# Twelve modulation blocks of the last mixer layer made in the even layer's attention instead of the recurrent layer

## The chip, the cores and the metric

The kernel runs on one core of one Trainium2 chip. The core has five engines that run side by side and wait for each other through semaphores: TensorE (PE, matmuls into the eight PSUM banks), VectorE (DVE), ScalarE (ACT), GpSimd (POOL) and SyncE (SP), which here issues the weight loads. The metric is the device time of one execution in microseconds, as the median of several.

## The reference

Everything is float32. A token stream x of 256 x 1024 goes through two blocks one after the other. The first has a recurrent mixer layer (a WKV-7 group of 8 heads of 64, and a gated delta rule group of 4 heads of 128, in chunks of 64 tokens), an MLP, a banded attention and a second MLP. The second block has an even mixer layer (neighbourhood attention on 8 heads and differential attention on 4 pairs of heads), a convolutional FFN, an odd mixer layer (grouped-query attention and a long convolution) and a last FFN; it also carries 256 context tokens. What matters here is how the second block is modulated:

```python
for layer in range(DEPTH):
    mod_l = (jax.nn.silu(c) @ w_ada[layer] + b_ada[layer])[:, None, :]
    mod_c = jax.nn.silu(c_ctx) @ w_ada[layer] + b_ada[layer]
    sh1_l, sc1_l, g1_l, sh2_l, sc2_l, g2_l = jnp.split(mod_l, 6, axis=-1)
```

`c` and `c_ctx` are inputs. So both layers' modulation vectors (6 x 1024 numbers for x and for the context) depend on nothing that the network computes and may be made at any time before their use. Layer 0's are first used when the second block starts, layer 1's only at the end of the FFN of layer 0, ahead of the odd mixer.

## The kernel before

**Weights.** All weights come from memory in blocks of up to 128 x 4096 numbers (2 MB) through a ring of three slots (`RING = 3`). `weight_plan` (L127) lists their order; SP issues them in that order, each as soon as PE has let go of the block three places earlier (L3292), and `weight` (L316) checks that PE takes them in that same order. An order changed in one place must be changed in the other.

**Modulation.** Each layer's `w_ada` is 12 blocks, `ada0` to `ada11` for layer 0 and `ada12` to `ada23` for layer 1. `pe_ada(j)` (L1021) multiplies one block by silu(c) and silu(c_ctx) with eight matmuls that use 32 columns of the array each, in four row strips; `dve_ada(j)` (L1032) adds the bank to the tile ADR. After twelve of them `pe_mod` (L1043) sums and turns ADR with four small matmuls, and `dve_mod` (L1051) adds the bias and writes the tile MODF. Their matmuls depend on nothing but the ring, and all 24 are written by hand between steps of the recurrent layer (`pe_mix`, `dve_mix`).

**The recurrent layer's end.** A triangular inverse is made in five steps k = 1 to 5 (L1353) for two groups g: matmuls "LX" (copied out by ACT), then "XLX" and "XLXt" (added by DVE, which then makes the masked operand of the next LX). Behind it come "ub" and "wb", and then four chunks c (L1378), each with `pe_bchunk_in` (state times queries) and `pe_bchunk_out` (state update and output), with DVE between the two. Blocks 11 to 16 stand in and behind the inverse, 17 to 23 in the chunks. Then `pe_eout` (L1996) turns the result y and multiplies it by the output projection, `pe_mod(1)` between the two.

**The even layer's attention.** `pe_pairs` (L753) runs 24 steps, twelve of neighbourhood attention (two with an added table and one without in each group of three, and an output product of 16 matmul records after each group) and twelve of differential attention. Step i issues the scores of step i, then what `between[i]` holds, then the transposes of step i-2 and the output product of step i-3. DVE (`dve_pairs`, L830) takes maxima, normalizes, copies half of the transposes; ACT takes exponentials and copies the other half.

**PSUM banks.** `open_bank` (L300) gives a result its bank. Without a number it takes the next in rotation, and in each case PE waits until the bank's last content has been read:

```python
            if b is None:
                b = state["bank"] % 8
                state["bank"] += 1
            if state["last"][b]:
                reader, n = marks.get("read " + state["last"][b], (scalar_done, 0))
                pe.wait_ge(reader, n)
```

In `pe_pairs` the scores have fixed banks 0 to 3, the transposes 4 to 6 and the outputs 7 (6 and 7 in the differential half), whatever the rotation stands at. Two scores are opened together before either is computed.

Of the kernel before, what the change touches and what calls it, by code (L numbers as in the profile page):

```python
# [126 lines left out]
def weight_plan():  # L127

    plan = []
    plan += [("lora_in", 8 * 256), ("rkv1", 4096), ("rkv0", 4096), ("lora_out", 3 * 512), ("rkv2", 4096)]  # L130
    ada = [(f"ada{j // 12}.{j % 12}", 4096) for j in range(24)]
    plan += [("bqkv0", 4096)] + ada[0:2] + [("bqkv1", 4096), ("bqkv2", 4096), ("bgate", 4096), ("bab", 64)] + ada[2:]
    plan += [(f"eout{i}", 4096) for i in range(2)]

    def mlp(i):
        return ([(f"up{i}.{n}", 4096) for n in range(8)] + [(f"down{i}.{h}.{n}", 4096) for n in range(4) for h in range(2)]
                + [(f"pproj{i}", 2048)] + [(f"pgate{i}.{h}", 4096) for h in range(2)])

    def ffn(i):
        return ([(f"cup{i}.{n}", 4096) for n in range(11)]  # L140
                + [(f"cdown{i}.{s}.{h}.{n}", 4096 if n < 2 else 3072) for s in range(2 - i) for n in range(3) for h in range(2)])

    plan += mlp(0) + [(f"qkv{i}", 4096) for i in range(6)] + [(f"aout{i}", 4096) for i in range(2)] + mlp(1)
    plan += [(f"win{i}", 4096) for i in (3, 4, 0, 1, 2, 5)] + [(f"wout{i}", 4096) for i in range(2)] + ffn(0)
    plan += [("hin1", 4096), ("hfilter", 3 * 64 + 1024), ("hin2", 4096), ("gq", 4096), ("gkv", 8 * 256), ("hin0", 4096)]
    plan += [(f"oout{i}", 4096) for i in range(2)] + ffn(1)
    return plan
# [65 lines left out]
def build(nc, T, out, counts):  # L213

    with ExitStack() as ctx:
# [64 lines left out]
        SM = small  # L280
# [966 lines left out]
        def pe_mix():  # L1247
# [105 lines left out]
            for k in range(1, 6):  # L1353
# [4 lines left out]
                if k < 3:  # L1358
                    pe_chunk_out(k + 1)
                pe_ada(10 + k)  # L1360
                for g in range(2):
                    pe_xlx("gdn", k, g, LX2, XT2)
                if k == 1:
                    pe_mod(0)
            pe_ada(16)
            pe.wait_ge(vector_done, at("gdn ready"))
# [11 lines left out]
            for c in range(4):  # L1378
                if c > 0:
                    pe_ada(16 + 2 * c)  # L1380
                    pe_bchunk_in(c)
                pe_ada(17 + 2 * c)
                pe_bchunk_out(c)
# [250 lines left out]
        def dve_mix():  # L1634
# [167 lines left out]
            for k in range(1, 6):  # L1802
                if k < 3:
                    dve.wait_ge(vector_done, dve.n)
                    dve_chunk_in(k + 1)
                    dve_chunk_out(k + 1)
                dve_ada(10 + k)
                for g in range(2):
# [23 lines left out]
            for c in range(4):  # L1832
                if c > 0:
                    dve_ada(16 + 2 * c)
                dve_bchunk_in(c)
                if c == 0:
                    dve_ada(16)
                if c == 1:
                    dve_y_affine()
                if c == 2:  # L1840
                    dve_y_out()
                dve_ada(17 + 2 * c)
                dve_bchunk_out(c)
                if c == 0:
                    dve_y_scale()
                dve.wait_ge(vector_done, dve.n)
# [13 lines left out]
            dve.mark("yb src")  # L1860
            dve_mod(1)

# [133 lines left out]
        def pe_eout():  # L1996
            ws, pss = [], {}
            for h, (Y, src) in enumerate(((YA, "ya src"), (YB, "yb src"))):
                pe.wait_ge(vector_done, at(src))
                for t in range(2):  # L2000
                    pe_turn(f"ymix turned {t}.{h}", [Y[:, t, i * P:(i + 1) * P] for i in range(4)])
                if h == 0:
                    pe_mod(1)
                for t in range(2):
# [306 lines left out]
        junk512 = ar.take(512)  # L2311
# [387 lines left out]
        def pe_even():  # L2699
# [61 lines left out]
            pe.wait_ge(loaded["bias"], at("bm loaded"))  # L2761
            pe_pairs("even", even_steps, PB5)

# [103 lines left out]
        def dve_even():  # L2867
# [66 lines left out]
            dve.wait_ge(vector_done, dve.n)  # L2934
            dve_pairs("even", even_steps, PB5, LAMR[:, 4:5], SM[:, 152:168], junk512)
            dve.mark("subln sums")
# [579 lines left out]
```

## Time and profile before

| | us |
|---|---|
| median of 3 runs | 2123.4 (2119.75 to 2123.53) |
| the profiled execution | 2126.54 |
| its span on the core | 2124.7 |
| mean granted clock, as a share of the full clock | 0.991 |

The profile is of one execution. Its span is the time between its first and last instruction, 1.8 us under that execution's time. Engine times are busy times inside the span: PE is the matmul side of TensorE, PEld its weight loads. A "releaser" is the event that ended an engine's wait. Matmuls are pipelined, a matmul appears as two records here, and their ends are modelled, so the starts carry more than the durations.

### The profile page before, as it was taken

The page shows a single profiled execution, that of the slowest core. Times are in us where ns is not written, and L with a number is a line of the kernel's source. Part 1 is how long each engine was busy: PE and PEld are TensorE (multiplying, and loading weights), DVE is VectorE, ACT ScalarE, POOL GpSimd, SP SyncE. Part 2 cuts the span into 40 slices and gives each one's busy share as a digit, 9 for nine tenths or more (in the row PEclk, how much of TensorE's full clock was granted, in tenths as well). Part 3 has the DMA queues.
Part 4 walks back from the last instruction along what each step waited for, and adds up shares of the span by engine and source line. Part 5 has one row for each costly group of instructions (what it writes and reads, how often), then busy time and mean ns, then how long its engine had stood idle before and what let it go on. Part 6 is the DMA issues. An engine that isn't in the chain of part 4 may idle for free.

```text
span 2124.7 us, 25115 instructions
## 1 busy us (share of the span) xinstructions
PE 2068.8 (97%) x10948; PEld 1468.0 (69%) x10948; DVE 1152.4 (54%) x1642; ACT 389.4 (18%) x787; POOL 10.8 (1%) x22
## 2 busy tenths in 40 slices
PE   8999999999999999999999999999999999999998
PEld 7887674895467589545864556988874466559963
DVE  2643765664521466643444764555555765646765
ACT  2313110100031410004112642111110012321110
POOL 0000000000000000000000000000000000000000
PEclk9999999999999999999999999999999999999999
DMA  5323777445343244534231102122223353124441
GB/s 199 120 120 131 296 268 328 178 178 214 138 177 140 80 174 159 188 148 163 80 119 40 40 1 80 45 110 84 108 91 138 148 212 139 40 80 159 159 163 75
DMA packets 22749, 292.69 MB, mean 138 GB/s; under 512 B 2752, under 2 KB 3008, under 8 KB 4848
## 3 DMA queue, kind: packets, MB, share of 16 engines
q1 hardware_dynamic: 20864, 280.67, 34.8%
q0 software_dynamic: 1776, 10.43, 1.3%
q8 instruction: 86, 1.41, 0.3%
q14 instruction: 23, 0.19, 0.0%
HBM read 290.03 MB, written 1.05 MB: 137 GB/s over the span
## 4 chain that ended last, share of the span: by engine, by line
PE 88%; DVE 8%; DMA 2%; ACT 1%; issue 1%; SPq 0%; DVEq 0%; ACTq 0%
PE bank L324 86%; DMA ring<-in_W 2%; PE bank L685 1%; DVE small L848 1%; DVE arena L869 1%; DVE arena L639 1%; DVE arena L862 0%; DVE arena L1016 0%; PE bank L778 0%; DMA X<-in_x 0%; DVE arena L2560 0%; DVE arena L696 0%; DVE arena L843 0%; DVE HT L2436 0%; DVE arena L488 0%
## 5 line engine op out<-in xcount | busy, mean ns | idle before, releaser
L324 PE MATMUL bank<-arena 128*128 128x128 f32 (+9 forms) x3856 | 679.5, 350 | 7.3 <-DVE arena L1008 2.5
L324 PEld LDWEIGHTS bank<-arena 128*128 128x128 f32 (+3 forms) x3856 | 474.3, 183 | 197.8 <-issue 159.0
L324 PE MATMUL bank<-HT,ring 128*128 128x128 f32 (+1 forms) x2672 | 453.7, 328 | 3.5 <-DMA ring<-in_W 1.8
L324 PEld LDWEIGHTS bank<-HT,ring 128*128 128x128 f32 x2672 | 403.6, 191 | 48.1 <-issue 9.5
L324 PE MATMUL bank<-ring,arena 128*128 128x512 f32 x690 | 307.4, 600 | 7.6 <-DVE arena L470 7.0
L324 PEld LDWEIGHTS bank<-ring,arena 128*128 128x128 f32 x690 | 131.4, 192 | 170.1 <-issue 169.8
L324 PE MATMUL bank<-ring,HT 128*128 128x512 f32 (+2 forms) x512 | 192.6, 533 | 2.4 <-DMA ring<-in_W 1.4
L324 PE MATMUL bank<-arena,ring 128*128 128x128 f32 (+2 forms) x1046 | 172.4, 322 | 0.8 <-issue 0.8
L694 ACT ACTIVATE arena<-bank 128x512 f32<-128x512 f32 (+2 forms) x127 | 69.7, 571 | 532.2 <-PE bank L324 502.0
L324 PEld LDWEIGHTS bank<-arena,ring 128*128 128x128 f32 (+1 forms) x1046 | 152.9, 191 | 13.9 <-issue 2.2
L324 PEld LDWEIGHTS bank<-ring,HT 128*128 128x128 f32 x512 | 89.3, 190 | 101.2 <-issue 95.9
L324 PE MATMUL bank<-HT,arena 128*128 128x128 f32 (+3 forms) x704 | 111.9, 323 | 0.0
L324 PEld LDWEIGHTS bank<-HT,arena 128*128 128x128 f32 (+1 forms) x704 | 98.3, 189 | 9.5 <-issue 2.6
L483 DVE TENSOR_TENSOR arena<-ring 128x2048 f32<-128x2048 f32 (+1 forms) x17 | 37.3, 2192 | 61.7 <-PE bank L324 61.7
L595 DVE TENSOR_TENSOR arena<-ring 128x2048 f32<-128x2048 f32 (+1 forms) x35 | 64.6, 1860 | 4.3 <-DMA ring<-in_W 4.0
L627 DVE TENSOR_TENSOR ADR<-ADR,bank 128x512 f32<-128x512 f32 x17 | 11.7, 688 | 89.9 <-PE bank L324 89.9
L2560 DVE SCALAR_TENSOR_TENSOR arena<-arena,CP 128x512 f32<-128x512 f32 (+1 forms) x88 | 54.4, 618 | 3.1
L632 DVE TENSOR_TENSOR arena<-ADR,bank 128x512 f32<-128x512 f32 x34 | 23.4, 687 | 58.4 <-PE bank L324 58.4
L324 PE MATMUL bank<-ring,SCW 128*32 128x512 f32 x384 | 50.7, 652 | 4.1 <-DMA ring<-in_W 3.4
L812 ACT ACTIVATE arena<-bank,small 128x512 f32<-128x512 f32 (+1 forms) x80 | 47.3, 599 | 35.4 <-DVE small L848 27.8
L616 ACT ACTIVATE arena<-bank 128x512 f32<-128x512 f32 x37 | 22.0, 595 | 159.1 <-PE bank L324 110.5
L778 PE MATMUL bank<-KC,arena 128*128 128x128 f32 x256 | 39.0, 282 | 10.7 <-DVE arena L862 5.2
(299 smaller groups left out, 1540.0 us busy)
## 6 DMA issues: line engine op xcount, KB each, us to landing
ring<-in_W SPq DMA_DIRECT2D x125, 2048.0 KB, 7.7
ring<-in_W SPq DMA_DIRECT2D x6, 1536.0 KB, 8.7
ring<-in_W SPq DMA_DIRECT2D x4, 1024.0 KB, 9.0
arena<-in_rel POOLq DMA_DIRECT2D x1, 2048.0 KB, 11.0
arena<-in_rpb POOLq DMA_DIRECT2D x1, 2048.0 KB, 9.2
arena<-in_dft POOLq DMA_DIRECT2D x2, 640.0 KB, 7.0
X<-in_x SPq DMA_DIRECT2D x2, 512.0 KB, 5.6
X<-in_ctx POOLq DMA_DIRECT2D x1, 1024.0 KB, 5.7
```

The costliest lines, as they stand in the source:

```text
L324: return nc.tensor.matmul(out_, lhsT, rhs, start=start, stop=stop, skip_group_check=True)
L483: tt(T1, B12, B11, ALU.subtract).then_inc(vector_done, dve.one())
L595: tt(d, a, b, op).then_inc(vector_done, dve.one())
L616: activation(dst, PS[banks.get(f"{label} {'x' if j == 1 else 'z'}{q}", 0)][:, :], ACT.Copy).then_inc(scalar_done, act.one())
L632: tt(dst, view(U), view(full(dve, f"{label} {c}{q}")[:, :]), ALU.add).then_inc(vector_done, dve.one())
L639: tt(dst, a, b, o).then_inc(vector_done, dve.one())
L685: last = nc.tensor.transpose(ps[:, i * P:(i + 1) * P], s, K("ident"))
L694: nc.scalar.activation(dst, s, ACT.Copy).then_inc(e.done, e.one())
L778: last = nc.tensor.transpose(ps[:, c * P:(c + 1) * P], PB[:, j % 3, s, a:a + P], K("ident"))
L812: activation(PB[:, i % 3, s, a:b], src, ACT.Exp, bias=st[:, c:c + 1], scale=sign, accum_out=st[:, 4 + c:5 + c]).then_inc(scalar_done, act. ...
L848: nc.vector.tensor_reduce(st[:, s * np_:(s + 1) * np_], ps[:, 0:w].rearrange("p (a c) -> p a c", a=np_), AX.X, ALU.max, negate=True).then_ ...
L2560: stt(c, raw[:, :, x:x + SEQ], C(f"fconv_w{i}", 22 * x + m), c, ALU.mult, ALU.add).then_inc(vector_done, dve.one())
```

## The change

The twelve blocks of layer 1 (`ada12` to `ada23`) leave the recurrent layer. `weight_plan` puts them between the last input weight of the even layer and the first output weight `wout0`. In `pe_pairs` and `dve_pairs` of the even attention they are handed in as `between`: blocks 12 and 13 in step 0, then one block each in steps 1, 2, 3, 4, 6, 7, 9, 10, 12 and 13. They take fixed banks, 7, and 6 for block 13. `pe_mod(1)` follows the attention on PE, `dve_mod(1)` on DVE. In the recurrent layer only `ada11` stays in the inverse, in step 1. The number of matmuls, of DVE instructions and of bytes loaded is the same as before.

```diff
@@ -129,7 +129,7 @@
     plan = []
     plan += [("lora_in", 8 * 256), ("rkv1", 4096), ("rkv0", 4096), ("lora_out", 3 * 512), ("rkv2", 4096)]
     ada = [(f"ada{j // 12}.{j % 12}", 4096) for j in range(24)]
-    plan += [("bqkv0", 4096)] + ada[0:2] + [("bqkv1", 4096), ("bqkv2", 4096), ("bgate", 4096), ("bab", 64)] + ada[2:]
+    plan += [("bqkv0", 4096)] + ada[0:2] + [("bqkv1", 4096), ("bqkv2", 4096), ("bgate", 4096), ("bab", 64)] + ada[2:12]
     plan += [(f"eout{i}", 4096) for i in range(2)]
 
     def mlp(i):
@@ -141,7 +141,7 @@
                 + [(f"cdown{i}.{s}.{h}.{n}", 4096 if n < 2 else 3072) for s in range(2 - i) for n in range(3) for h in range(2)])
 
     plan += mlp(0) + [(f"qkv{i}", 4096) for i in range(6)] + [(f"aout{i}", 4096) for i in range(2)] + mlp(1)
-    plan += [(f"win{i}", 4096) for i in (3, 4, 0, 1, 2, 5)] + [(f"wout{i}", 4096) for i in range(2)] + ffn(0)
+    plan += [(f"win{i}", 4096) for i in (3, 4, 0, 1, 2, 5)] + ada[12:] + [(f"wout{i}", 4096) for i in range(2)] + ffn(0)
     plan += [("hin1", 4096), ("hfilter", 3 * 64 + 1024), ("hin2", 4096), ("gq", 4096), ("gkv", 8 * 256), ("hin0", 4096)]
     plan += [(f"oout{i}", 4096) for i in range(2)] + ffn(1)
     return plan
@@ -1357,12 +1357,12 @@
                     pe_lx("gdn", k, g, MASKED2, XI2)
                 if k < 3:
                     pe_chunk_out(k + 1)
-                pe_ada(10 + k)
+                if k == 1:
+                    pe_ada(11)
                 for g in range(2):
                     pe_xlx("gdn", k, g, LX2, XT2)
                 if k == 1:
                     pe_mod(0)
-            pe_ada(16)
             pe.wait_ge(vector_done, at("gdn ready"))
             for t in range(2):
                 ps = open_bank(f"ub{t}")
@@ -1377,9 +1377,7 @@
                 pe.mark(f"wb{t}")
             for c in range(4):
                 if c > 0:
-                    pe_ada(16 + 2 * c)
                     pe_bchunk_in(c)
-                pe_ada(17 + 2 * c)
                 pe_bchunk_out(c)
 
         def act_keep(n, i, dst, h):
@@ -1804,7 +1802,8 @@
                     dve.wait_ge(vector_done, dve.n)
                     dve_chunk_in(k + 1)
                     dve_chunk_out(k + 1)
-                dve_ada(10 + k)
+                if k == 1:
+                    dve_ada(11)
                 for g in range(2):
                     dve_grow("gdn", k, g, XI2, XT2)
                     if k < 5:
@@ -1830,16 +1829,11 @@
                 copy_out(dve, f"wb{t}", WT[:, 4 * t:4 * t + 4, :], lambda ps: k4(ps[:, :]))
             dve.wait_ge(vector_done, dve.n)
             for c in range(4):
-                if c > 0:
-                    dve_ada(16 + 2 * c)
                 dve_bchunk_in(c)
-                if c == 0:
-                    dve_ada(16)
                 if c == 1:
                     dve_y_affine()
                 if c == 2:
                     dve_y_out()
-                dve_ada(17 + 2 * c)
                 dve_bchunk_out(c)
                 if c == 0:
                     dve_y_scale()
@@ -1858,7 +1852,6 @@
             dve.wait_ge(vector_done, dve.n)
             tt(YB, YB, GB, ALU.mult).then_inc(vector_done, dve.one())
             dve.mark("yb src")
-            dve_mod(1)
 
 
         def pe_norm_sum(label, tiles):
@@ -1999,8 +1992,6 @@
                 pe.wait_ge(vector_done, at(src))
                 for t in range(2):
                     pe_turn(f"ymix turned {t}.{h}", [Y[:, t, i * P:(i + 1) * P] for i in range(4)])
-                if h == 0:
-                    pe_mod(1)
                 for t in range(2):
                     pe.wait_ge(scalar_done, at(f"read ymix turned {t}.{h}"))
                 for t in range(2):
@@ -2759,7 +2750,15 @@
                     spread("kn")
             pe.wait_ge(vector_done, at("even heads"))
             pe.wait_ge(loaded["bias"], at("bm loaded"))
-            pe_pairs("even", even_steps, PB5)
+            blocks = {i: [12 + n] for n, i in enumerate((0, 1, 2, 3, 4, 6, 7, 9, 10, 12, 13), 1)}
+            blocks[0].insert(0, 12)
+
+            def modulation(i):
+                for n, j in enumerate(blocks[i]):
+                    pe_ada(j, 7 - n)
+
+            pe_pairs("even", even_steps, PB5, {i: lambda i=i: modulation(i) for i in blocks})
+            pe_mod(1)
 
             w = weight("wout0").rearrange("p (k c) -> p k c", k=KT)
             pss = [open_bank(f"wout0.{t}") for t in range(4)]
@@ -2932,7 +2931,15 @@
             dve.wait_ge(vector_done, dve.n)
             ts(LAMR[:, 4:5], LAMR[:, 4:5], -(0.8 - 0.6), None, ALU.add).then_inc(vector_done, dve.one())
             dve.wait_ge(vector_done, dve.n)
-            dve_pairs("even", even_steps, PB5, LAMR[:, 4:5], SM[:, 152:168], junk512)
+            rows_of = {i: 12 + n for n, i in enumerate((0, 1, 2, 3, 4, 6, 7, 9, 10, 12, 13), 1)}
+
+            def modulation(i):
+                if i == 0:
+                    dve_ada(12)
+                dve_ada(rows_of[i])
+
+            dve_pairs("even", even_steps, PB5, LAMR[:, 4:5], SM[:, 152:168], junk512, {i: lambda i=i: modulation(i) for i in rows_of})
+            dve_mod(1)
             dve.mark("subln sums")
             dve.wait_ge(scalar_done, at("subln root"))
             nc.vector.reciprocal(SM[:, 152:168], SM[:, 152:168]).then_inc(vector_done, dve.one())
```

## Rows read from the trace of the kernel before

**Rows 1.** Part 1 of the page: busy us (share of the span) x instructions.

```profile
PE 2068.8 (97%) x10948; PEld 1468.0 (69%) x10948; DVE 1152.4 (54%) x1642; ACT 389.4 (18%) x787; POOL 10.8 (1%) x22
```

**Rows 2.** Windows of four stages: length, busy by engine, PEclk, DMA share, GB/s.

```profile
284.00:309.00 25.00, 22.50 (x184) 17.54 (x176) 19.12 (x29) 2.99 (x5) 0.00 (x0) 1.00 0.68 252
319.00:348.00 29.00, 27.73 (x217) 14.52 (x216) 20.92 (x32) 0.00 (x0) 0.00 (x0) 0.94 1.00 422
1169.00:1216.00 47.00, 45.67 (x258) 25.79 (x256) 37.33 (x88) 29.78 (x87) 0.00 (x0) 1.00 0.13 46
1216.00:1253.00 37.00, 31.81 (x209) 21.77 (x210) 32.76 (x101) 24.89 (x73) 0.00 (x0) 1.00 0.01 1
```

**Rows 3.** Tile SCW, whole run: durations min/median/max in ns, starts, forms.

```profile
L324 PE MATMUL bank<-ring,SCW x384: 592/592/1063, 94.1 to 346.5; 128*32 128x512 f32 x192
```

**Rows 4.** PE's timeline around inverse steps: start, us, instructions, [idle before].

```profile
300.39 1.92 PE L324 MATMUL bank<-ring,SCW 128*32 128x512 f32 x16
302.25 3.84 PE L324 MATMUL bank<-arena 128*128 128x128 f32 x32
306.28 1.16 PE L324 MATMUL bank<-arena 128*128 128x128 f32 x8 [0.19 <-DVE arena L1008]
...
315.23 1.16 PE L324 MATMUL bank<-X,arena 128*128 128x128 f32 x8 [0.31 <-DVE arena L1016]
```

**Rows 5.** Chain that ended last, 260 to 370: start, us, what.

```profile
308.06 1.23 DVE small L1573
...
313.29 0.69 DVE ADR L1040
...
328.68 11.04 DMA ring<-in_W
...
343.40 11.57 DMA ring<-in_W
...
355.01 10.57 PE bank L324 x24
```

**Rows 6.** DVE's lines of code in 319 to 348: count, busy us, mean ns.

```profile
L1040 DVE TENSOR_TENSOR ADR<-ADR,bank 128x512 f32<-128x512 f32 x8 | 5.5, 687 | 6.3 <-PE bank L324 5.9
```

**Rows 7.** PE's timeline, the end of the recurrent layer.

```profile
339.77 3.56 PE L324 MATMUL bank<-ring,SCW 128*32 128x512 f32 x16 [0.87 <-DMA ring<-in_W]
...
348.02 1.09 PE L685 MATMUL bank<-KC,arena 128*128 128x128 f32 x8
```

**Rows 8.** PE's timeline in the even attention.

```profile
1169.56 1.13 PE L324 MATMUL bank<-arena 64*128 64x512 f32 x4
...
1175.41 1.09 PE L778 MATMUL bank<-KC,arena 128*128 128x128 f32 x8 [0.45 <-DVE arena L869]
...
1183.62 1.39 PE L778 MATMUL bank<-KC,arena 128*128 128x128 f32 x8
...
1216.40 0.66 PE L778 MATMUL bank<-KC,arena 128*128 128x128 f32 x4 [0.95 <-DVE arena L862]
```

**Rows 9.** DVE's timeline in the even attention.

```profile
1220.98 1.29 DVE L848 TENSOR_REDUCE small<-bank 128x1 f32<-128x512 f32 x2 [1.73 <-PE bank L324]
```

**Rows 10.** DMA issues in 1165 to 1185: KB each, us to landing.

```profile
ring<-in_W SPq DMA_DIRECT2D x1, 2048.0 KB, 7.6
```

**Rows 11.** Timelines around the band attention: PE twice, then ACT.

```profile
700.30 1.58 PE L324 MATMUL bank<-arena 64*128 64x256 f32 x16
...
731.41 19.12 PE L324 MATMUL bank<-ring,arena 128*128 128x512 f32 x44 [0.57 <-ACT arena L694]
...
700.40 0.60 ACT L694 ACTIVATE arena<-bank 128x512 f32<-128x512 f32 x1 [7.54 <-PE bank L324]
```

**Rows 12.** Timelines ahead of the GQA attention: PE, then DVE.

```profile
1837.07 13.24 PE L324 MATMUL bank<-arena 64*128 64x512 f32 x52
...
1838.24 0.87 DVE L3194 SCALAR_TENSOR_TENSOR arena<-bank,CP,arena 128x255 f32<-128x255 f32 x2 [2.29 <-PE bank L324]
1839.14 0.87 DVE L3198 SCALAR_TENSOR_TENSOR arena<-bank,CP,arena 128x255 f32<-128x255 f32 x2
```

## Prediction

> **What bounds the kernel now.** I read the totals first: TensorE is called busy for 2068.8 of 2124.7 us, VectorE for 1152.4 [rows 1]. A share that high says only that a stage must be read from inside, so next come the windows of the two places that the change touches [rows 2]. In the inverse's steps (284 to 309) PE is busy 22.5 of 25.0 us and DVE 19.12. In the four chunk steps (319 to 348) PE is busy 27.73 of 29 us, DVE 20.92, and the DMA share is 1.00 at 422 GB/s: the stream of weight blocks is full there. In the first half of the even attention (1169 to 1216) PE is busy 45.67 of 47 us and DVE 37.33; in the second half PE has 31.81 and DVE 32.76 of 37, and the DMA engines are almost still (46 and 1 GB/s). So the blocks leave a place where the DMA engines are full and go to one where they are empty. The question is whether PE has room there. The timelines and the chain of waits answer that, and after them the waits for PSUM banks.
>
> **What one block costs.** Each of the 24 blocks is 8 matmuls (16 records) of 592 ns, overlapping each other [rows 3]. Start to start a block takes PE 302.25 - 300.39 = 1.86 us [rows 4]. On DVE it is one add of 687 ns [rows 6].
>
> **Removed from the inverse.** In steps 2, 3 and 4 a block stands between the LX and the XLX matmuls. PE's waits lie elsewhere, before the next LX, 0.19 us on DVE [rows 4], so nothing late is uncovered: the copies of LX on ACT take about 0.6 us, and LX of group 1 and XLX of group 0 cover them. DVE's products come 1.86 us earlier with PE's. Each block is worth 1.86: 5.6 us. After step 4 DVE does the mean and variance of y from 308.06 until the add of block 15 at 313.29, an add of 0.69 [rows 5]. That work does not shrink, so blocks 15 and 16 give only about 0.7 us. The matmuls of "ub0", at 315.23 before [rows 4], start about 6.3 us earlier, at 308.9.
>
> **Removed from the chunk steps.** Blocks 17 to 23 go. Of DVE's 20.92 us [rows 2], 5.5 are eight adds [rows 6]; 15.4 remain. DVE waits for PE's products four times (two state products and two "vn" or "ob", about 1.15 us each, estimated as half of a PE piece of the 27.73 us: 4.6 in all); two copies of 0.7 lie beside PE; the handovers make some 1.0. That is 15.4 + 4.6 - 1.4 + 1.0 = 19.6 us where there were 29.0. The stage turns from bound by blocks to bound by DVE; gain 9.4 more, 15.7 in all. Behind it, the transposes of y (348.02 before [rows 7]) start at about 332.3. Then the waits for DMA go: the chain of waits runs through the ring for 11.04 us before 339.7 and for 11.57 before 355 [rows 5], and the output projection starts its second weight only at 355.01. With eout0, eout1 and up0.0 fetched early, the projection's first half ends about 17.4 us earlier than before. This holds another 1.7 us for two short waits and the `pe_mod` of four small matmuls. DVE's norm of YB then ends at about 340, the half projection at 348, so it stays covered. Bounds: 12 us (only the 6.3, and the chunk steps kept at DVE's pace of 20.92 plus 4.6) and 19 us. **Recurrent layer: -17.4.**
>
> **Added to the attention.** Twelve blocks. Are they in gaps? In the first twelve steps PE's pieces follow each other without idle but for 0.45 us at 1175.41 [rows 8]; transposes that stretch to 1.39 us instead of 1.09 [rows 8] hide about 0.3 more, in each of three groups. So a block is paid nearly in full. Ten blocks stand in steps 0 to 10: 10 x 1.86 = 18.6, less 0.45 and 3 x 0.3: 17.25. Blocks 22 and 23 stand in steps 12 and 13, where PE waited 0.95 us for DVE before the transposes at 1216.40 [rows 8]; they fill that, and DVE, which had 1.73 us of idle before 1220.98 [rows 9], takes its two adds without loss: 3.7 - 0.95 - 0.55 (stretched transposes, PE and DVE drawn side by side) = 2.2, plus 0.3 because block 23 wants bank 7 before DVE has read block 22: 2.5. No block beside attention steps is in this trace, so the bounds are wide: DVE's 0.69 each (8.3 us) if PE had room, 1.92 each plus waits (23 us) if not. I take the upper end, as the PE rows show no room.
>
> **The ring in the attention.** It has three slots. Blocks 12 and 13 are there at step 0, which starts at 1169.56 [rows 8]. Block 14 takes the slot of win5, free at that moment, and one load alone takes 7.6 us from issue to landing [rows 10]: 1177.2. Scores with a table take two pieces like the 1.13 us of 1169.56 (1.06 start to start), those without one, so step 1 ends its scores at 1169.56 + 2.1 + 3.7 + 2.1 = 1177.4, just after. Block 15 is issued when block 12 is done (1173.5), and the DMA engines need about 5.0 us a block when full (2.1 MB at 422 GB/s [rows 2]). It lands near 1182.2 but is wanted at 1177.4 + 1.86 + 1.06 = 1180.3: 1.9 us, with 0.1 for block 16. Later ones are in time, since a step and its block take at least 5.0 us. **+2.0** (0 to 4). `pe_mod(1)` then stands alone on PE before wout0: **+0.9**. DVE's add of the bias runs beside wout0. Sum for the attention: 17.25 + 2.5 + 2.0 + 0.9 = **+22.6**.
>
> **What is moved without being named: PSUM banks.** `open_bank` hands out banks in rotation and waits for the last reader. Thirteen rotating opens go before the even attention (blocks 12 to 23 and mod1), and one comes back after it. So every rotating bank is 3 further on between eout and wout0, and 4 further on after. Among themselves that changes nothing; it matters where a fixed bank follows, in `pe_pairs`. Counted through the program, three places change. (a) Band attention: the second score bank (1) is now that of "v1.0", copied by ACT from 700.40 for 0.60 us, while the scores started at 700.30 [rows 11]: +0.75. The first output bank is no longer that of the last head, for which PE waited 0.57 us at 731.41 [rows 11]: -0.6. (b) Even attention: wout0 opens banks 4 to 7, 7 being the last output that DVE reads; `pe_mod` covers it: 0. (c) GQA attention: bank 1 is now that of "hu.1", which DVE reads in the convolution until 1839.14 + 0.87 = 1840.0, while PE's scores started at 1837.07, the head of 13.24 us without a gap [rows 12]: **+2.9** (between 0, if PE catches up in its later waits, and 3.0). I take the top, since DVE's next waits are for PE. Together **+3.1**.
>
> **Sum.** -17.4 + 22.6 + 3.1 = **+8.3 us**. The profiled run took 2126.5 us (span 2124.7), 3.1 over the median of 2123.4; the difference is applied to the median: **2131.7 us**, 0.39% slower.
>
> **Rivals.**
> A. *The blocks are hidden in the attention* (the other side). DVE is nearly as full as PE there (37.33 of 47 us), and if PE's busy time is stretched by the way its ends are modelled, a block costs DVE's 0.69: 8.3 + 0.9 = 9.2 instead of 22.6, so -5.1: 2118.3. It decides when a block costs under about 0.8 us. For it: LDWEIGHTS are far from full, 25.79 of 47 us [rows 2]. Against: PE's pieces start one behind the other with no idle but what is named above [rows 8]. The Trainium skill bears on this: its page Perfetto Trace Analysis (section Identifying the Most-Contended Engine) holds that matmul busy time is a poor measure and that LDWEIGHTS' share shows the headroom. By that rule the attention has 45% free, and this rival would be right. Chance 0.07.
> B. *The bank and ring waits come to nothing*: PE's later gaps in GQA take up the wait, and block 15 lands in time. 8.3 - 3.1 - 2.0 = +3.2: 2126.6. For it: one load's 7.6 us is a single sample. Chance 0.17.
> C. *PE's clock falls where the fillers go.* The granted clock stood at half level (1.2 of 2.4 GHz) when block 22 ran, 3.56 us for 1.92, after a short wait for DMA [rows 7]; that 1.6 us is in my gain. In the chunk steps PE would be busy some 70% with gaps of up to 2 us. If it falls there, PE's 4.6 us on the path double and the projection's start loses 1.6: +6.2 on top of 8.3: 2137.9. Against: in the second half of the even attention, with PE at 31.81 of 37 us, the granted clock is 1.00 [rows 2]. The Trainium skill, page TensorE: Matmul & The Clock Gate (section HAM oscillation), warns that gaps between groups of matmuls let the clock fall, so that fillers are worth more than their time. [...] Chance 0.18.
> Forecast: 0.58. That the change does not do what it says is excluded by the code: all twelve blocks leave.
>
> **Numbers.** Within 0.2% is 4.2 us, about what a measurement of this kernel can tell from no change: 2119.2 to 2127.6. The forecast and C are slower (0.76), B is the same (0.17), A faster (0.07). The range leaves out A and covers B, C and the bounds of the ring and of the chunk steps: 2124.5 to 2139.
>
> **What would show it.** In the profile after: "ub0" about 6 us earlier; the chunk steps at 20 us; no DMA wait from 280 to 350; then the start of the even attention 17 us earlier (less 0.15), its length 84 to 105 us; a wait of 2 us on the ring at step 2; and a wait of PE on DVE's convolution of 2.9 us ahead of the GQA scores. What would make it wrong: a block in the attention that costs much less than 1.86, a longer wait on the ring, or a half clock in either place.

## The result and the profile after

The changed kernel takes 2144.35 us (median of four executions, 2140.44 to 2144.99) against 2123.47 us for the kernel before beside it (2119.75 to 2124.13): ratio 1.0098, interval 1.0081 to 1.0116, or +20.9 us. Forecast were +8.3 us and a range that ended at 2139. The direction was right, the size was not. The profiled execution took 2140.44 us (span 2138.6), 13.9 us over that of before.

The totals say little, as [rows 1] did: the same work in a longer span.

```profile
PE 2070.5 (97%) x10948; PEld 1473.0 (69%) x10948; DVE 1154.7 (54%) x1642; ACT 390.1 (18%) x787; POOL 10.7 (1%) x22
```

The windows of the four stages (columns as in [rows 2]): inverse steps, chunk steps, first and second half of the even attention.

```profile
284.00:304.00 20.00, 17.20 (x140) 15.87 (x138) 18.39 (x27) 4.87 (x7) 0.00 (x0) 1.00 0.01 1
312.73:333.46 20.73, 16.10 (x104) 13.88 (x105) 15.51 (x24) 0.00 (x0) 0.00 (x0) 0.84 0.00 1
1153.60:1207.00 53.40, 50.58 (x329) 23.06 (x328) 34.21 (x73) 22.27 (x63) 0.00 (x0) 1.00 0.90 364
1207.00:1261.50 54.50, 49.28 (x337) 30.10 (x336) 46.17 (x131) 33.39 (x95) 0.00 (x0) 1.00 0.38 146
```

The DMA stream has moved: from 1.00 in the chunk steps to 0.00, and from 0.13 in the attention to 0.90. The chunk steps last 20.7 us where they lasted 29 [rows 2, 7], and DVE is busy 15.5 us of them, as worked out (15.4). But their mean granted clock is 0.84 where it was 0.94, as a share of 2.4 GHz; half clock is the lower of its two levels, 1.2 GHz. PE's timeline of the recurrent layer's end (start, us, instructions, [idle before <- releaser]) shows where:

```profile
276.36 8.90 PE L324 MATMUL bank<-arena 64*64 64x64 f32 x112
...
300.70 3.00 PE L324 MATMUL bank<-arena 128*128 128x128 f32 x24 [0.64 <-DVE arena L1008]
307.26 1.90 PE L324 MATMUL bank<-X,arena 128*128 128x128 f32 x8 [3.55 <-DVE arena L1016]
308.96 1.91 PE L324 MATMUL bank<-arena 128*128 128x128 f32 x8
310.66 1.17 PE L324 MATMUL bank<-X,arena 128*128 128x128 f32 x8
...
313.96 4.06 PE L324 MATMUL bank<-arena 64*128 64x128 f32 x32 [1.24 <-DVE arena L1610]
320.19 3.13 PE L324 MATMUL bank<-arena 64*128 64x128 f32 x16 [2.17 <-DVE arena L1613]
323.95 5.96 PE L324 MATMUL bank<-arena 128*64 128x128 f32 x32 [0.63 <-DVE arena L1627]
330.51 3.02 PE L324 MATMUL bank<-arena 128*64 128x128 f32 x24 [0.60 <-DVE arena L1627]
333.46 1.09 PE L685 MATMUL bank<-KC,arena 128*128 128x128 f32 x8
...
349.21 1.04 PE L685 MATMUL bank<-KC,arena 128*128 128x128 f32 x8
```

"ub0", the piece at 307.26, takes 1.90 us where it took 1.16 [rows 4]: behind a wait of 3.55 us PE works at half clock, and again behind one of 2.17 us. No wait in these rows is for DMA any more. I measure this **recurrent stage** from the first piece behind mod0 to the transposes of YB: 349.21 - 276.36 = 72.85 us. Before, in the rows below, it was 365.42 - 277.78 = 87.64. So it gave 14.8 us.

```profile
277.78 5.13 PE L324 MATMUL bank<-arena 64*64 64x64 f32 x80
...
365.42 1.04 PE L685 MATMUL bank<-KC,arena 128*128 128x128 f32 x8
```

PE's timeline of the even attention, after:

```profile
1153.61 1.13 PE L324 MATMUL bank<-arena 64*128 64x512 f32 x4
1154.67 1.13 PE L324 MATMUL bank<-arena,KC 128*128 128x256 f32 x4
1155.73 3.64 PE L324 MATMUL bank<-ring,SCW 128*32 128x512 f32 x32
...
1161.66 1.92 PE L324 MATMUL bank<-ring,SCW 128*32 128x512 f32 x16 [0.17 <-DMA ring<-in_W]
1163.51 1.14 PE L324 MATMUL bank<-arena 64*128 64x256 f32 x8
1166.54 1.93 PE L324 MATMUL bank<-ring,SCW 128*32 128x512 f32 x16 [1.89 <-DMA ring<-in_W]
...
1177.44 1.92 PE L324 MATMUL bank<-ring,SCW 128*32 128x512 f32 x16 [0.68 <-DMA ring<-in_W]
...
1220.29 1.93 PE L324 MATMUL bank<-ring,SCW 128*32 128x512 f32 x16 [0.45 <-DVE ADR L1040]
...
1260.59 0.98 PE L324 MATMUL bank<-KC,ADR 128*128 128x32 f32 x8
1261.55 0.67 PE L324 MATMUL bank<-ring,arena 128*128 128x512 f32 x1
```

From its first scores to wout0 it lasts 1261.55 - 1153.61 = 107.94 us. Before, it lasted 1252.81 - 1169.56 [rows 8] = 83.25 us, so +24.7. Of the rows below, the second is the start of wout0 before; the first is the longest wait of its second half.

```profile
1248.09 0.66 PE L778 MATMUL bank<-KC,arena 128*128 128x128 f32 x4 [1.36 <-DVE arena L862]
...
1252.81 3.60 PE L324 MATMUL bank<-ring,arena 128*128 128x512 f32 x8
```

The ring wait of 1.89 us at step 2 is where it was expected. Those of 0.17 at step 1 and 0.68 at step 4 were not expected; with 0.15 ahead of block 16 they make 2.9 us. The last place is the GQA attention, PE and then DVE:

```profile
1849.14 14.88 PE L324 MATMUL bank<-arena 64*128 64x512 f32 x52 [3.02 <-DVE arena L3205]
```

```profile
1848.12 0.87 DVE L3205 SCALAR_TENSOR_TENSOR arena<-bank,CP,arena 128x255 f32<-128x255 f32 x2
```

The wait for the bank is 3.02 us (forecast 2.9), but the piece behind it takes 14.88 us where it took 13.24 [rows 12]: half clock again, 1.64 us more. In the band attention a wait of 0.78 us came and 0.63 us went, 0.15 in all. Sum of the stages: -14.8 + 24.7 + 4.7 + 0.15 = +14.8 us (the two profiles differ by 13.9). That leaves two questions: are the terms right when each is done alone, and why do the medians lie 20.9 us apart and the profiles 13.9?

### The profile page after: what moved, and what is told of

It is laid out like the page before. It is cut to its first block, busy times and chain, and to the rows that moved or that the text cites. A ratio compares the mean times of both kernels' runs of the same rounds, so it can differ in the third digit from the quotient of the medians.

```text
span 2138.6 us, 25116 instructions
## 1 busy us (share of the span) xinstructions
PE 2070.5 (97%) x10948; PEld 1473.0 (69%) x10948; DVE 1154.7 (54%) x1642; ACT 390.1 (18%) x787; POOL 10.7 (1%) x22
## 4 chain that ended last, share of the span: by engine, by line
PE 88%; DVE 8%; DMA 2%; ACT 1%; issue 1%; SPq 0%; DVEq 0%; ACTq 0%
PE bank L324 86%; DMA ring<-in_W 2%; PE bank L685 1%; PE bank L778 1%; DVE small L848 1%; DVE arena L639 1%; DVE arena L1016 0%; DVE arena L862 0%; DMA X<-in_x 0%; DVE arena L2551 0%; DVE arena L696 0%; DVE arena L843 0%; DVE arena L869 0%; DVE HT L2427 0%; DVE arena L488 0%
## 5 line engine op out<-in xcount | busy, mean ns | idle before, releaser
L324 PEld LDWEIGHTS bank<-arena,ring 128*128 128x128 f32 (+1 forms) x1046 | 153.0, 191 | 15.4 <-issue 3.7
L778 PEld LDWEIGHTS bank<-KC,arena 128*128 128x128 f32 x256 | 27.1, 141 | 32.3 <-DVE arena L862 10.1
```

The lines of the kernel that those rows point to most:

```text
L324: return nc.tensor.matmul(out_, lhsT, rhs, start=start, stop=stop, skip_group_check=True)
L778: last = nc.tensor.transpose(ps[:, c * P:(c + 1) * P], PB[:, j % 3, s, a:a + P], K("ident"))
```

## The experiments

Twelve runs were made, in four groups, two of them of kernels already measured; ratios are to the kernel before on the same chip, whose medians there were 2126.5, 2126.4, 2125.5 and 2125.2 us.

**The change again, and its parts alone.** First the changed kernel unchanged, as the measure for the others.

> The changed kernel once more. Its profiled execution took 2140.4 us, the three others 2143.8 to 2145.0, with a mean granted clock of 0.986 where the profile has 0.990. Theory 1 (where TensorE stands at half clock differs from execution to execution, and more of it comes with the change): profile and median differ again by some us, and the time follows the mean granted clock. Theory 2 (the profiled execution is the rule and the others were disturbed): all come near 2140.

Measured: 2144.53 us, ratio 1.0082 (1.0067 to 1.0097), +18.1 us. The GQA wait is 3.02 us again with 14.89 us behind it. So the change costs 18.1 us in one measurement and 20.9 in the other, with intervals that overlap.

Second, the banks moved back to where they were in the kernel before (here and below, ... marks lines left out of a diff):

```diff
+                if h == 0:
+                    state["bank"] += 13
...
             pe_mod(1)
+            state["bank"] -= 1
```

> The change with the bank rotation set forward by 13 behind the first transposes of the output projection and back by 1 ahead of wout0, so that every rotating bank is what it was in the kernel before. No instruction is added. Theory 1 (the wait of 3.0 us before the GQA scores comes from the shifted rotation, and the half clock after it too): that wait is gone, time 3.0 to 4.7 us under the changed kernel, and the band attention loses its 0.8 us wait and gets back the one of 0.6 behind it. Theory 2 (PE's later gaps would have taken the wait up): no change beyond 0.5 us.

Measured: 2142.59 us, ratio 1.0071 (1.0047 to 1.0095). The GQA scores start without a wait and take 13.24 us, so the wait was the banks' doing. The total, 1.9 us under e1 where 3.0 to 4.7 were expected, can't be told from that of e1. The edit put mod1 in wout0's first bank, and the ring wait in the attention (3.12 us) had a half clock behind it, which e1's attention didn't have. A better version is e5.

Third, the recurrent half alone: the blocks leave and are made nowhere (layer 1 is modulated with layer 0's vector), banks as before.

> Only the first half of the change: the twelve blocks leave the recurrent layer and are not made anywhere (layer 1 is modulated with layer 0's vector, so this part of the computation is left out); bank rotation as before from the output projection on. Theory 1 (the prediction's sum): 16 to 17.4 us under the kernel before. Theory 2 (the clock falls for long without the blocks between, in executions that the profile did not catch): 8 to 12 us under it, with a mean granted clock under 0.990.

Measured: 2110.42 us, ratio 0.9929 (0.9912 to 0.9945), **-16.0 us**, for a forecast of -17.4. The stage is 346.68 - 273.85 = 72.83 us, as in the changed kernel, with the same half clock behind the same waits.

Fourth, the attention half alone: the kernel before, and the twelve blocks made a second time in the attention.

```diff
-    plan += [(f"win{i}", 4096) for i in (3, 4, 0, 1, 2, 5)] + [(f"wout{i}", 4096) for i in range(2)] + ffn(0)
+    plan += [(f"win{i}", 4096) for i in (3, 4, 0, 1, 2, 5)] + [(f"again1.{q}", 4096) for q in range(12)] + [(f"wout{i}", 4096) for i in range(2)] + ffn(0)
...
```

> Only the second half: the kernel before, which still makes the twelve blocks in the recurrent layer, makes the same twelve again in the even attention, at the places of the change, with their loads and the four small matmuls behind them. Banks in rotation as before. Theory 1 (a block is paid in full on PE, and the ring and one bank add some 3 us): 23 to 25 us over the kernel before. Theory 2 (a half clock follows the ring's wait in executions other than the profiled one): 26 to 30 us over it. Theory 3 (the blocks are half hidden): 9 to 15.

Measured: 2153.05 us, ratio 1.0122 (1.0102 to 1.0143), **+26.6 us**. PE waits 2.77 us for the ring at step 2, and 0.70 us ahead of wout0 that are this edit's own (the first row and the last):

```profile
1185.91 1.92 PE L324 MATMUL bank<-ring,SCW 128*32 128x512 f32 x16 [2.77 <-DMA ring<-in_W]
...
1280.69 3.67 PE L324 MATMUL bank<-ring,arena 128*128 128x512 f32 x8 [0.70 <-DVE MODF L1063]
```

So the halves are -16.0 and +25.9. With the 4.8 us of the banks they add up to 14.7, as the stages above do to 0.1; e1 measured 18.1, and the intervals of the parts are too wide to say that 3.4 us are missing. e4's time lies in the range of its second theory, but no half clock followed the ring wait here, and the mean granted clock of its executions is that of the kernel before (0.9915). The rival of hidden blocks (+9.2 for the attention) is out.

Here an added block cost PE 1.74 of its 1.86 us ((108.48 - 83.25 - 2.77 - 0.70 - 0.9)/12, the stage being 1280.69 - 1172.21 = 108.48 us). The Trainium skill, page Perfetto Trace Analysis (section Identifying the Most-Contended Engine), takes LDWEIGHTS' busy share, with the share of the peak rate, as the measure of TensorE's headroom. By LDWEIGHTS' share (25.79 of 47 us [rows 2]) the attention was 45% free, and the trace doesn't agree.

**One cause each.** e5 is the changed kernel with banks aligned and `pe_mod(1)` in a bank of its own:

```diff
-            pe_mod(1)
+            pe_mod(1, 4)
```

> The change with all rotating banks as in the kernel before (as in the second experiment), and the four small matmuls of pe_mod(1) in the fixed bank 4, so that wout0 doesn't wait for DVE to read them (0.7 us in the second experiment). It is the base for the next two. Theory 1 (bank waits cost 3 to 4.6 us): the changed kernel less 3.5 to 5, so about 14 us over the kernel before on the same chip. Theory 2 (the banks cost nothing in the end): 18 over.

Measured: 2139.49 us, ratio 1.0060 (1.0047 to 1.0074), +13.1: 5 us under e1 (about 14 over the kernel before was expected). Of these, 3.0 is the wait and 1.6 the half clock behind it; the intervals overlap. Now the clock: 28 filler matmuls in the waits of the emptied recurrent layer.

```diff
+            pe_fill(12, ADR[:, 0:P])
             pe.wait_ge(vector_done, at("gdn ready"))
...
                     pe_bchunk_in(c)
+                pe_fill((4, 7, 0, 1)[c], ADR[:, 0:P])
                 pe_bchunk_out(c)
+                pe_fill((0, 2, 2, 0)[c], ADR[:, 0:P])
```

> The same with 28 small matmuls (128x128 by 128x128, results unused) put into PE's waits of the recurrent layer's end: 12 ahead of ub0 where PE waits 3.55 us, then 4, 7, 2, 2 and 1 in the chunk steps. They depend on nothing. Theory 1 (PE's clock falls there because PE pauses, and costs 2.6 us or more): the granted clock stays full from 300 to 335, the stage is 2 to 4 us shorter and so is the time. Theory 2 (the clock falls for other reasons): half clock stays in the stage, time the same or up to 1 us longer.

Measured: 2137.04 us, ratio 1.0044 (1.0027 to 1.0061), 2.5 us under e5, with intervals that overlap; the trace is clearer. "ub0" is back at its full speed behind a wait of only 0.87 us, and the stage is 352.40 - 281.71 = 70.69 us instead of 72.83. It has no half clock.

```profile
281.71 8.90 PE L324 MATMUL bank<-arena 64*64 64x64 f32 x112
...
308.89 2.84 PE L324 MATMUL bank<-ADR 128*128 128x128 f32 x24
312.61 1.16 PE L324 MATMUL bank<-X,arena 128*128 128x128 f32 x8 [0.87 <-DVE arena L1016]
...
315.39 1.06 PE L324 MATMUL bank<-arena 128*128 128x128 f32 x8
...
336.65 1.09 PE L685 MATMUL bank<-KC,arena 128*128 128x128 f32 x8
...
352.40 1.04 PE L685 MATMUL bank<-KC,arena 128*128 128x128 f32 x8
```

The attention (108.75 us) has a half clock too: behind a ring wait of 1.90 us the block took 3.44 us. Now the ring: e5 with blocks 14 to 23 computed from block 13's slot, not loaded (what they should add is left out).

> The same as the base, but blocks 14 to 23 in the attention are computed from the slot of block 13 and not loaded (layer 1's modulation is then made from the wrong weights; this part of the computation is left out). The matmuls and adds are all there. Theory 1 (ring waits of 2.9 to 3.5 us, sometimes followed by a half clock of 3.4 us that costs 1.7): 3 to 5 us under the base. Theory 2 (another wait takes their place): within 1 us of it. The rest of the attention then shows the price of a block alone: 1.86 us by theory.

Measured: 2137.24 us, ratio 1.0051 (1.0037 to 1.0065), 2.3 us under e5 where 3 to 5 were expected, with intervals that overlap. The attention is 1261.63 - 1156.98 = 104.65 us, against 109.0 in e5: late loads cost 4.3 us there, 2.68 of them e5's wait at step 2, the rest mostly the half clock behind it.

**Fewer blocks moved.** e8: blocks 12 to 18 stay, 19 to 23 go to steps 12, 13, 15, 17 and 19, where PE waits for DVE. The sum of blocks 12 to 18 is not kept until then, so layer 1's vector is left incomplete.

```diff
+            moved = {12: 19, 13: 20, 15: 21, 17: 22, 19: 23}
```

> A smaller move: blocks 12 to 18 stay in the recurrent layer (12 to 16 where they were, 17 ahead of the first chunk's output, 18 between the second chunk's two halves), only 19 to 23 go to the even attention, to its differential half (steps 12, 13, 15, 17, 19), where DVE and not PE sets the pace. Banks in rotation as before. Theory 1 (a block there costs about DVE's add, 0.7 to 0.9 us, and the recurrent layer still loses its waits for the ring, 10 us): 3 to 5 us under the kernel before. Theory 2 (a block costs 1.86 there too, and the ring's waits are only part of it): 0 to 4 us over it.

Measured: 2131.52 us, ratio 1.0021 (1.0009 to 1.0033), +5. The 3 to 5 us of gain that I expected didn't come, because the recurrent stage took 360.93 - 279.65 = 81.28 us, with half clock from 334 to 346, behind this:

```profile
333.49 2.61 PE L324 MATMUL bank<-arena 128*64 128x128 f32 x16 [2.37 <-DVE arena L1629]
```

The attention was 1255.48 - 1165.07 = 90.4 us, so a block costs 1.27 us there ((7.15 - 0.8)/5), not 1.86.

**What an execution is, and better places.** The kernel before with a second profile:

> The kernel before, unchanged, with a second profile. It tells what in a profile-to-profile difference is the program and what is the execution. Theory (the rest of the difference is time at half clock in code that the change does not touch): the ratio is 1.000; the stages that the change touches repeat to 0.2 us where the granted clock is full (from the XLX piece behind mod0 to the transposes of YB 87.6 us, the even attention from its first scores to wout0 83.25 us), and the spans of the two profiles differ by about half of the difference of their time at half clock (39.5 us in the first profile). Rival (the stages themselves wander, by DMA waits): the recurrent stage differs by over 1 us between the two profiles at the same clock.

Measured: ratio 0.9995 (0.9981 to 1.0009). Its profile, the view of the span and the mean granted clock, beside that of the first profile:

```profile
core 0: 2114.4 us, clock 0.996
```

```profile
core 0: 2124.7 us, clock 0.991
```

The same program is 10.3 us shorter. The stages repeat: the attention is 83.25 us in both, the recurrent stage 358.17 - 270.79 = 87.38 us and 87.64. Added up over windows of 2 us, PE is 34.2 us at half clock in the first profile and 13.6 us in the second (both without some 6 us at the end, with no matmul left). Half of the difference is 10.3 us, so the clock accounts for the whole difference of these two profiles.

The second profile has no half clock in the recurrent stage, where the first had 3.4 us of it (block 22 [rows 7]), and the stage is only 0.26 us shorter. What the slower block took, the ring hid: the waits for it in the stage add up to 4.0 us in the second profile and 2.7 in the first.

e10 is e8 with the first sum kept by a `pe_mod` of its own and with fillers in the chunk steps:

```diff
+                pe_fill((0, 0, 7, 1)[c], K("ident"))
                 pe_bchunk_out(c)
+                pe_fill((0, 1, 2, 0)[c], K("ident"))
```

> Blocks 12 to 18 stay in the recurrent layer and are summed there by a pe_mod of their own in the output projection; blocks 19 to 23 are made in steps 12, 13, 15, 17 and 19 of the even attention and added to it. Banks aligned as before. Filler matmuls on a constant stand in the waits of the chunk steps (7 and 1 ahead of the output of chunks 2 and 3, 1 and 2 behind that of chunks 1 and 2), to hold the granted clock where e8_keep7 had half clock from 334 to 346. Theory (what the emptied waits lose is clock, what the attention costs is PE time): the recurrent stage falls to 79 us (81.3 in e8_keep7 less 3 to 5 us of the doubled pieces, plus 0.9 for the extra small product): -8.5 against before; the attention +7.2; 0 to 2 us faster than before, about 2126.4 less 1. Rival (the spread of the clock elsewhere rules): the stages come out as said and the median does not follow, 3 to 5 us slower as e8_keep7. Rival (fillers delay the chunk steps as much as they save): stage at 81 to 82, 1 us slower.

Measured: 2126.28 us, ratio 0.9997 (0.9986 to 1.0008), not to be told from no change. The stage is 358.06 - 277.17 = 80.89 us, not 79. Seven fillers stood ahead of work that was ready, and the gap that had let the clock fall lay one piece earlier, with a half clock still behind it:

```profile
331.00 2.40 PE L324 MATMUL bank<-arena 128*64 128x128 f32 x16 [1.96 <-DVE arena L1637]
333.33 2.99 PE L324 MATMUL bank<-KC 128*128 128x128 f32 x14
336.25 2.17 PE L324 MATMUL bank<-arena 64*128 64x128 f32 x16
```

e11 is e6 without a block in step 2:

```diff
-            blocks = {i: [12 + n] for n, i in enumerate((0, 1, 2, 3, 4, 6, 7, 9, 10, 12, 13), 1)}
+            blocks = {i: [12 + n] for n, i in enumerate((0, 1, 3, 4, 6, 7, 9, 10, 12, 13, 15), 1)}
...
```

> e6_fill with one edit: no block in step 2 of the even attention; blocks 14 to 23 stand in steps 1, 3, 4, 6, 7, 9, 10, 12, 13 and 15. Theory (the ring wait of 1.9 to 2.8 us at step 2 and the half clock behind it come from three blocks wanted within 11 us while one load takes 7.6 us): the wait at that place falls below 0.7 us, no half clock behind it; the attention is 103 to 104.5 us long from its first scores to wout0 instead of 107 to 109; 4 us less than e6_fill, +6 us against before (about 2132.5). Rival (the ring is just as late one step further on, as the stream is full): the wait moves to step 3 with over 1.5 us, and the time is that of e6_fill, 2137.

Measured: 2131.04 us, ratio 1.0027 (1.0015 to 1.0038), +5.5 where e6 had +10.7, with intervals that just overlap. The block of step 3 has no ring wait, and the attention is 1258.89 - 1154.71 = 104.18 us (108.75 in e6).

```profile
1167.52 1.13 PE L324 MATMUL bank<-arena,KC 128*128 128x256 f32 x4
1168.64 1.93 PE L324 MATMUL bank<-ring,SCW 128*32 128x512 f32 x16
```

Last, the blocks only where PE waits anyway. Block 19 fills the gap that e10 showed, and only four move, at least four steps apart:

```diff
+                if c == 2:
+                    pe_ada(19)
                 if c > 0:
                     pe_bchunk_in(c)
...
+            moved = {12: 20, 16: 21, 20: 22, 24: 23}
```

> Blocks 12 to 19 stay in the recurrent layer: 17 and 18 ahead of the output of chunks 0 and 1, 19 ahead of the state product of chunk 2, where e10_keep7_fill showed PE waiting 1.96 us for DVE with a half clock after it. No filler but 2 matmuls behind chunk 2 (the 7 of e10 stood in front of work that was ready: 2.99 us). Only blocks 20 to 23 move, to steps 12, 16, 20 and 24 of the even attention, at least four steps apart, step 24 being behind the last scores, where PE waits 1.36 us for DVE. Banks aligned. Theory (a block is nearly free only where PE waits for DVE and DVE has time for its add): no half clock from 300 to 345; the recurrent stage (87.4 us in the kernel before, 80.9 in e10) becomes 77.8 us, -9.6; the attention costs 0.9 + 0.8 + 0.8 + 0.5 and 0.8 for the small product, 83.25 + 3.8 = 87.1 us; sum -5.8: 2120 us, ratio 0.9973. Rival (DVE is the bound of both places, so each add of 0.69 us and each late PE piece is paid in full): stage 79.5, attention 83.25 + 4 x 1.27 + 0.8 = 89.1; sum -2.0, ratio 0.999. Rival (the ring: blocks 17 to 19, eout0 and eout1 again wanted faster than one in 5 us): a wait on the ring between 320 and 350, stage above 82, no gain.

Measured: **2120.03 us, ratio 0.9975 (0.9965 to 0.9985), -5.1 us: faster than the kernel before**, and so than the changed one. PE's timeline, recurrent stage and then attention:

```profile
276.82 5.13 PE L324 MATMUL bank<-arena 64*64 64x64 f32 x80
...
328.21 1.93 PE L324 MATMUL bank<-ring,SCW 128*32 128x512 f32 x16
330.65 4.21 PE L324 MATMUL bank<-arena 128*64 128x128 f32 x32 [0.52 <-DVE arena L1639]
...
355.13 1.04 PE L685 MATMUL bank<-KC,arena 128*128 128x128 f32 x8
...
1159.26 1.13 PE L324 MATMUL bank<-arena 64*128 64x512 f32 x4
...
1239.81 1.93 PE L324 MATMUL bank<-ring,SCW 128*32 128x512 f32 x16
1241.67 0.66 PE L778 MATMUL bank<-KC,arena 128*128 128x128 f32 x4
...
1246.78 13.98 PE L324 MATMUL bank<-ring,arena 128*128 128x512 f32 x32
```

Block 19 at 328.21 turns a wait of 1.96 us into one of 0.52, and no piece from 300 to 345 is stretched. The stage is 78.31 us (-9.2 against the mean of the two profiles of before), the attention 87.52 (+4.3); the block at 1239.81 fills the wait of 1.36 us that the kernel before and the changed kernel had there. The two stages make -4.9 of the -5.1 us. A moved block costs (4.27 - 0.8)/4 = 0.87 us. The edit changes the number of blocks and their places at once, so what each is worth alone isn't shown.

## Where the prediction was right and where it was not

The second question first: how the executions split by clock. For each, span times mean granted clock is what it would last if half clock never occurred; the rest is what half clock took. The split is rough, and it puts too much on the clock, since it also halves the time in which PE only waits: the 10.2 us at half clock in the emptied stage count 5.1 here, and e6 gave back 2.1.

| kernel (executions) | mean granted clock | span x clock, mean us | the rest, us |
|---|---|---|---|
| before, beside the others (67) | 0.9918 | 2106.8 | 17.4 |
| before, e9 (10) | 0.9922 | 2107.0 | 16.6 |
| after, with e1 (8) | 0.9871 | 2114.1 | 27.6 |
| e2 (5) | 0.9868 | 2111.3 | 28.3 |
| e3, emptied recurrent layer (4) | 0.9892 | 2085.3 | 22.7 |
| e5 (6) | 0.9882 | 2112.4 | 25.3 |
| e7 (4) | 0.9865 | 2106.4 | 28.8 |
| e8 (12) | 0.9879 | 2103.1 | 25.7 |
| e4, recurrent layer as before (4) | 0.9915 | 2132.0 | 18.3 |
| e6, gaps filled (4) | 0.9908 | 2114.0 | 19.7 |
| e10 (12) | 0.9911 | 2105.0 | 18.9 |
| e11, gaps filled (12) | 0.9918 | 2111.1 | 17.4 |
| e12 (9) | 0.9919 | 2100.9 | 17.2 |

**The failed step: the clock.** The forecast put PE's clock in the emptied recurrent layer at nothing and left it to rival C, with a chance of 0.18 and a price of 6.2. The runs showed half clock there in every kernel with the holes. It cost 2.1 us of the stage (72.83 to 70.69 with e6's 28 fillers) and 1.6 us more behind the GQA wait, where C hadn't looked. The stages' own times, at full clock, make -16.9 + 24.7 + 3.0 + 0.15 = +11.0 us where 8.3 was forecast, and these 3.8 us bring that to +14.8. By the executions the change costs 7.3 us at full clock and 10.2 us of half clock. That the 7.3 comes so near to 8.3 is chance: the forecast was 2.7 us short of the stages at full clock.

Two steps led to it. C's argument against itself, that PE at 31.81 of 37 us keeps its clock in the second half of the attention [rows 2], was the wrong row: there the waits are mostly 0.3 to 0.5 us, with one of 0.95 and one of 1.36, while the emptied layer has single waits of 3.55 and 2.17 us. And the working had such a wait in hand: blocks 15 and 16 were found to stand beside DVE's mean and variance, and "only about 0.7 us" was counted for them, without asking what PE does in the hole of 3.5 us that they leave. C priced the chunk steps; of the 2.1 us, 1.6 lay in the four pieces ahead of them (5.47 us, in e6 316.45 - 312.61 = 3.84).

Kernels with single waits of over 2 us in the recurrent layer lose 22.7 to 28.8 us to the clock by the table, those without them 16.6 to 19.7. The Trainium skill, page TensorE: Matmul & The Clock Gate (section HAM oscillation), describes matmul groups shorter than the wait behind them, after which the next group starts cold. The trace agrees for the wait of 3.55 us, which follows a piece of 3.00 us. Behind the wait of 2.17 us, which follows 4.06 us of work, there was half clock too, which that description doesn't cover.

Over half of the 10.2 us has a place. The stage is at half clock for 10.2 us in every profile with the holes (13.6 in e1; 3.4 and 0 in those of before), and the piece behind the GQA wait for 3.4 us in the two profiles of the changed kernel and in none with aligned banks. Counted by halves as in the table, that is 6 to 8 us more than before; in time only the 3.8 us above are shown. The rest lies in stretches that the change doesn't touch (12 to 22, 100 to 114, 200 to 210, 1600 to 1700 and others) and differs from one execution to the next: 30.8 and 13.6 us at half clock outside the touched stages in the profiles of before, 23.9 and 33.7 in those of the changed kernel. The profiles don't tell whether that is the change's doing; why the medians lie 3 to 6 us further apart than the stages' +14.8 stays open. The profiled execution of the changed kernel had clock 0.990, its other three 0.986, and so the profiles lie only 13.9 us apart.

**Recurrent layer, -17.4 forecast, -14.8 in the profile, -16.0 alone.** "ub0" came 6.5 us earlier in the stage (6.3 forecast), with no DMA wait behind it. The four pieces from "ub0" on took 5.47 us where the sum left them at 3.84, and the chunk steps 20.7 us for 19.6. Filled and at full clock (e6) the chunk steps still took 336.65 - 316.45 = 20.2 us, so about 0.6 of the 1.1 us is DVE's pace, sized too short, and 0.5 the clock. The output projection gave 1.65 us (1.7 forecast). The 1.6 us of half clock before, which C counted as part of the gain, was worth 0.26 us: e9's stage without it is 87.38 us.

**Attention, +22.6 forecast, +24.7 in the profile, +25.9 alone.** Ring waits 2.9 us for 2.0 (2.77 in one piece in e4), `pe_mod` 0.8 to 1.0 for 0.9, and 20.9 us for twelve blocks (24.7 - 2.9 - 0.9), where 17.25 + 2.5 = 19.75 stood. A block is paid nearly in full there; the credits for gaps and stretched transposes were together too large by about 1.1. The ring was late at step 4 too (0.68 us), where the working took a step and its block to be long enough for a load.

**Banks, +3.1 forecast, +4.8 in the profile.** The wait came at the place and with the size worked out (3.02 us for 2.9), ahead of the band scores 0.78 for 0.75. With the ring waits of 2.9 us that leaves nothing of rival B, and the clock added 1.6.

**The range** reached 2139: it took C alone as its end and no term beside it. The misses had one sign and add up: clock 3.8, ring 0.9, blocks 1.1, the recurrent layer's pace 0.5, and the 3 to 6 us that stay open.

## What to carry to other kernels

Work that looks like filler may hold the granted clock: before it is taken out, look for the single longest wait that it covers (3.55 us here), not at the busy share of the stage. A moved piece of work is cheap only where the engine waits and the reader of its result has room, one piece to a gap: 0.87 us a block in e12 where the full move paid 1.74 (20.9/12). And a load that is moved must be counted against the ring: giving step 2 no block took 4.6 us off the attention (108.75 us in e6, 104.18 in e11), with the half clock behind its wait.

## What the runs showed of the hardware

I had not expected how short a wait is enough. Behind single waits of PE of 1.90 us (e6, attention), 1.96 us (e10) and 2.37 us (e8) the next pieces ran at half clock, but not each time: behind 1.89 us in the changed kernel's attention and 2.77 us in e4 they did not. Nor had I expected that the program's own spread is mostly this: over the 77 executions of the kernel before, mean granted clock and time correlate with -0.86, from 0.989 to 0.996 and from 2116 to 2131 us.
